# The second projection of a squared-ReLU MLP by seven block products in six of its eight chunks, on one core

## The reference, cut to what matters

```python
def squared_relu_mlp(x, w1, w2):
    return jnp.square(jax.nn.relu(x @ w1)) @ w2
...
x = x + squared_relu_mlp(rms_norm(x, mlp_norm[i]), mlp_w1[i], mlp_w2[i])
```

## Time and profile before

| what | value |
|---|---|
| time, median of 3 executions | 2232.59 us (2228.85 to 2233.13) |
| time of the profiled execution | 2230.44 us |
| its span | 2228.6 us |
| TensorE (PE) busy | 2059.4 us, 92% |
| VectorE (DVE) busy | 1388.8 us, 62% |
| ScalarE (ACT) busy | 978.0 us, 44% |
| GpSimd (POOL) busy | 328.4 us, 15% |
| mean granted TensorE clock | 0.969 of full speed |

### The profile page before, as it was taken

How to read it: one execution, slowest core, us unless ns; L and a number is a source line. 1 busy time by engine, 2 the same in 40 slices (tenths; PEclk the granted TensorE clock), 3 DMA queues, 4 the chain that set the end, 5 groups by cost and what they waited for, 6 DMA issues and landing times. The chain is left out here.

```text
span 2228.6 us, 28924 instructions
## 1 busy us (share of the span) xinstructions
PE 2059.4 (92%) x10963; PEld 1081.8 (49%) x10963; DVE 1388.8 (62%) x1507; ACT 978.0 (44%) x1257; POOL 328.4 (15%) x291
## 2 busy tenths in 40 slices
PE   7998988889399999999967999959899999999999
PEld 5445436644244544554435565544444444444444
DVE  5135227743789999999978452384696456555544
ACT  5122126732378888888856352272332212121210
POOL 0000021000123233233300000032020011011100
PEclk9999999999699999999988999979999999999999
DMA  6111220041289999999974552235202201210201
GB/s 269 38 38 39 67 57 1 1 180 79 106 349 415 408 413 406 395 399 409 390 288 181 174 193 80 79 91 187 76 1 76 76 38 38 75 75 0 75 0 76
DMA packets 74722, 353.03 MB, mean 158 GB/s; under 512 B 16336, under 2 KB 23120, under 8 KB 42064
## 3 DMA queue, kind: packets, MB, share of 16 engines
q1 hardware_dynamic: 56304, 305.21, 35.1%
q0 software_dynamic: 18336, 46.69, 6.5%
HBM read 326.67 MB, written 29.36 MB: 160 GB/s over the span
## 5 line engine op out<-in xcount | busy, mean ns | idle before, releaser
L413 PE MATMUL ps<-split,xt 128*128 128x512 f16 x928 | 353.9, 381 | 25.3 <-DMA xt<-arena 19.8
L414 PE MATMUL ps<-split,xt 128*128 128x512 f16 x928 | 353.8, 381 | 0.0
L415 PE MATMUL ps<-split,xt 128*128 128x512 f16 x928 | 353.7, 381 | 0.0
L544 DVE SCALAR_TENSOR_TENSOR split<-stage,split 128x2048 f16<-128x2048 f32 x128 | 289.4, 2282 | 5.7 <-ACT split L540 4.0
L540 ACT ACTIVATE split<-stage 128x2048 f16<-128x2048 f32 x128 | 240.5, 1904 | 94.4 <-PE ps L415 94.4
L413 PE MATMUL ps<-xt,split 128*128 128x512 f16 (+1 forms) x660 | 239.7, 363 | 9.9 <-issue 8.3
L414 PE MATMUL ps<-xt,split 128*128 128x512 f16 (+1 forms) x660 | 239.7, 363 | 0.0
L415 PE MATMUL ps<-xt,split 128*128 128x512 f16 (+1 forms) x660 | 239.4, 363 | 0.0
L413 PE MATMUL ps<-split,arena 128*128 128x512 f16 x512 | 194.1, 379 | 0.3 <-DVE resid L1901 0.3
L414 PE MATMUL ps<-split,arena 128*128 128x512 f16 x512 | 194.0, 379 | 0.0
L415 PE MATMUL ps<-split,arena 128*128 128x512 f16 x512 | 194.0, 379 | 0.0
(11 more groups left out here) (383 smaller groups left out, 3628.9 us busy)
## 6 DMA issues: line engine op xcount, KB each, us to landing
stage<-in_w_gate SPq DMA_DIRECT2D x64, 1024.0 KB, 7.5
stage<-in_w_up SPq DMA_DIRECT2D x64, 1024.0 KB, 7.9
arena<-in_w_down SPq DMA_DIRECT2D x64, 1024.0 KB, 7.9
stage<-in_w_mlp SPq DMA_DIRECT2D x32, 1024.0 KB, 6.3
arena<-in_conv_taps POOLq DMA_DIRECT2D x32, 576.0 KB, 4.3
stage<-in_w_dense_a SPq DMA_DIRECT2D x16, 1024.0 KB, 7.3
stage<-in_w_dense_b SPq DMA_DIRECT2D x12, 1024.0 KB, 9.6
resid<-in_x SPq DMA_DIRECT2D x16, 512.0 KB, 4.5
```

Source lines behind the costliest of these rows:

```text
L413: nc.tensor.matmul(out_ap, lh, rh, start=start, stop=False)
L414: nc.tensor.matmul(out_ap, lh, rl, start=False, stop=False)
L415: return nc.tensor.matmul(out_ap, ll, rh, start=False, stop=stop)
L544: nc.vector.scalar_tensor_tensor(out=wlo(s), in0=wstage(s), scalar=WS, in1=whi(s), op0=ALU.mult, op1=ALU.subtract).then_inc(s_wo[s], 1)
```

## The change

In chunks 1 to 6 the down part becomes a seven-product scheme too. Its operands are, on the side of the hidden features, the blocks `A11`, `A12`, `A22` (names of their place) and the sums `S1` to `S4` of blocks, and on the side of the weights `B11`, `B21`, `B22` and the sums `T1` to `T4`. Chunk 7 keeps a plain down part. What changes in detail:

- **TensorE.** A down part has 28 groups of 6 matmuls (7 products by 4 tiles) in place of 16 groups of 12. The bank of each is given by `DOWN_BANK`; a group waits for the read of its bank's last use (`bank_reader`), and the first group of each product also for the operands.
- **Weight operands.** The up and the down part each have seven, and share a ring of seven buffers (`RING`), so that an operand of one part may be written only when the product that used the buffer in the other part is done. `mlp_hi` and `mlp_lo` go out of chunks 1 to 7.
- **GpSimd.** Per chunk it has four more weight sums (`down_sums`), four sums of hidden blocks (`hidden_sums`) and the low parts of these four, 128 x 1024 each. At the end, in chunk 7, it has six sums of 128 x 2048.
- **VectorE.** The blocks of the result are not all added to `resid`. Three running sums `E_V`, `E_X`, `E_Y` take the products that several blocks share; GpSimd adds them to `resid` in chunk 7. There are 32 reads of a bank per down part in place of 16. `relu_square` and `hidden_lo` are 128 x 1024 in place of pairs of 128 x 512. `bank_sum` is a scalar_tensor_tensor that scales by `IWS`.
- **SyncE.** The two units of the up part and the two of the down part go to the same two `stage` slots. Those of the down part are loaded when the seven up operands are split, those of the next up part when the seven down operands are split.

```diff
+        DOWN_ORDER = ["B11", "B21", "T4", "T3", "B22", "T2", "T1"]
+        SUMS = [split[:, 12288:16384].bitcast(F32), stage[:, 4096:6144], stage[:, 6144:8192]]
+        H_OF = {"B11": "A11", "B21": "A12", "T4": "A22", "T3": "S3", "B22": "S4", "T2": "S2", "T1": "S1"}
+        DOWN_TO = {"B11": (H11, E_V), "B21": (H11,), "T4": (H21,), "T3": (E_X,), "B22": (H12,), "T2": (E_V,),
+                   "T1": (E_Y,)}
+        UP_BANK = [0, 1, 2, 3, 0, 1, 3]
+        DOWN_BANK = [0, 2, 1, 3, 2, 1, 0, 1, 2, 3, 0, 1, 2, 3]
...
+            def body(c):
+                for down in range(2):
+                    for s in range(2):
...
+                            sp.wait_ge(s_pl, 14 * (c - 1) + 7 * down)
+                        src = a["w_mlp"][bass.ds(SLOTS * c + 2 * down + s, 1), :, :].rearrange("o p c -> (o p) c")
+                        sp.dma_start(wstage(s), src).then_inc(s_wl[s], 16)
...
+            def hidden_sums(c):
+                pool.wait_ge(s_relu, 8 + 4 * (c - 1) + 4)
+                pool.wait_ge(s_ml, 8 + 3 * (c - 1) + 3)
+                add(U_X, U_V, U_X, ALU.add, s_hs)
+                pool.wait_ge(s_hs, 4 * (c - 1) + 1)
+                add(U_V, U_W, U_V, ALU.subtract, s_hs)
+                add(U_W, U_X, U_W, ALU.subtract, s_hs)
+                pool.wait_ge(s_hs, 4 * (c - 1) + 3)
+                add(U_Y, U_Y, U_W, ALU.subtract, s_hs)
+                pool.wait_ge(s_hs, 4 * (c - 1) + 4)
+                for name in ("S3", "S4", "S2", "S1"):
+                    pool.wait_ge(s_mh, 8 + 7 * (c - 1) + H_HI.index(name) + 1)
+                    add(h_slot(name)[:, 1024:2048], HQ[name], h_slot(name)[:, 0:1024], ALU.subtract, s_hp)
+
+            up_sums(1)
+            with pool.Fori(1, NC - 1) as c:
+                down_sums(c)
+                hidden_sums(c)
+                up_sums(c + 1)
+            pool.wait_ge(s_mr, PER * (NC - 2))
+            for n, (to, v0, v1) in enumerate([(H12, H12, E_V), (H12, H12, E_Y), (E_X, E_X, E_V), (H21, H21, E_X),
+                                            (E_X, E_X, E_Y), (H22, H22, E_X)]):
...
+                add(to, v0, v1, ALU.add, s_pool)
...
+                hidden_hi("A22")
...
+                    op_hi(act, 1, "T2", c)
+                    op_hi(act, 1, "T1", c)
+                    op_hi(act, 0, "A11", c + 1)
+                    hidden_hi("S3")
+                    hidden_hi("S4")
+                    hidden_hi("S2")
+                    hidden_hi("S1")
+                    for name in W_UP[1:]:
+                        op_hi(act, 0, name, c + 1)
...
+                    read("P5b", f)
+                    bank_sum(U_V, f, 6, U_V, "P3")
+                relu_square("A21", "P3")
...
+                    op_lo(dve, 1, "T1", c)
+                    for g in range(28):
+                        down_read(g)
+                        if g == 5:
+                            op_lo(dve, 0, "A11", c + 1)
+                        if g == 9:
+                            op_lo(dve, 0, "A12", c + 1)
+                        if g == 20:
+                            op_lo(dve, 0, "A22", c + 1)
+                    for name in W_UP[3:]:
+                        op_lo(dve, 0, name, c + 1)
...
+                    for g in range(28):
+                        name = DOWN_ORDER[g // 4]
+                        h, w = h_slot(H_OF[name]), w_slot(1, name)
+                        if g % 4 == 0:
+                            pe.wait_ge(s_pl, w_count(1, name, c))
+                            if H_OF[name] in H_LO_N:
+                                pe.wait_ge(s_hp, 4 * (c - 1) + H_LO_N[H_OF[name]])
...
+                        pe.wait_ge(s_mr, PER * (c - 1) + bank_reader(g))
```

More of the change, by code:

```diff
@@ L690, in build @@
[L690 to L694, removed]
+        RING = [split[:, 2048 * i:2048 * i + 2048] for i in range(4)] + [
+            Z[:, 0:1024].bitcast(F16), junk[:, :].bitcast(F16), Z[:, 1280:2304].bitcast(F16)]
+        W_UP = ["A11", "A12", "A22", "S2", "S3", "S1", "S4"]
+        W_DOWN = ["B11", "B21", "B22", "T4", "T3", "T2", "T1"]
@@ new lines, in build @@
+        W_LAST = ["B11", "B21", "B22", "B12"]
+        W_FROM = {"A11": (0, 0), "A12": (1, 0), "A22": (1, 1), "S2": (0, 0), "S3": (0, 1), "S1": (1, 1), "S4": (1, 0),
+                  "B11": (0, 0), "B21": (0, 1), "B12": (1, 0), "B22": (1, 1),
+                  "T3": (1, 1), "T1": (1, 0), "T2": (0, 0), "T4": (0, 1)}
+        SUM_N = {"S1": 1, "S3": 2, "S2": 3, "S4": 4, "T3": 1, "T1": 2, "T2": 3, "T4": 4}
+        UP_ORDER = W_UP
+        DOWN_ORDER = ["B11", "B21", "T4", "T3", "B22", "T2", "T1"]
@@ L1923, in _ @@
                 if j in (8, 9, 10):
-                    op_lo(dve, ("A11", "A12", "A22")[j - 8], 1)
+                    op_lo(dve, 0, W_UP[j - 8], 1)
                 if j in (11, 13):
@@ L1952, in body @@
                 for f in range(2):
                     dve.wait_ge(s_ua, 2 * (c - 1) + 1 + f)
-                    bank_sum(U_W, f, 1, U_V)
+                    bank_sum(U_W, f, 1, U_V, "P2")
+                relu_square("A11", "P2")
+                hidden_lo("A11")
+                for name in ("B11", "B21", "B22"):
+                    op_lo(dve, 1, name, c)
+                if last:
+                    op_lo(dve, 1, "B12", c)
                 for f in range(2):
-                    summed(0, f)
@@ L1965, in body @@
+                relu_square("A12", "P4")
+                hidden_lo("A12")
+                if not last:
+                    op_lo(dve, 1, "T4", c)
+                    op_lo(dve, 1, "T3", c)
+                for f in range(2):
+                    bank_sum(U_X, f, 5, U_X, "P5")
+                for f in range(2):
+                    bank_sum(U_V, f, 5, U_V, "P5b")
+                relu_square("A22", "P5")
+                hidden_lo("A22")
                 if not last:
-                    op_lo(dve, "A11", c + 1)
+                    op_lo(dve, 1, "T2", c)
@@ new lines, in body @@
+                if last:
+                    hidden_lo("A21")
+                    for j in range(8, 24):
+                        dve.wait_ge(s_pool, 4 + (0 if j < 16 and j % 2 == 0 else 2 if j < 16 else 6))
+                        down_sum(j, G_DOWN + j // 4 - 1)
+                else:
+                    op_lo(dve, 1, "T1", c)
[9 more added lines that the diff above has]
+                        op_lo(dve, 0, name, c + 1)
```

380 lines of the change are left out of this document (207 added, 173 removed).

## The result

The changed kernel takes 2265.22 us (median of 4 executions, 2262.03 to 2265.81), the kernel before 2232.05 us on the same chip (4 executions, 2228.85 to 2233.13): a ratio of 1.0148, 95% interval 1.0131 to 1.0166. It is 33 us slower. The forecast was 2257 us, the range 2238 to 2272. The profiled execution took 2265.81 us, its span is 2264.0 us.

What follows compares the result with a forecast made beforehand. TensorE's matmuls were taken to bound the MLP, with only TensorE's waits added. From 2230.4 us, plus 6.0 for six looped chunks (78.7 us each) and 20.2 for chunk 7, it forecast 2257 us, range 2238 to 2272.

Steps and rivals of the forecast that it cites:

- Sign and mechanism: Whole kernel: slower, chance 0.82, through TensorE's waits as GpSimd and VectorE take turns on SBUF operands.
- 24 matmuls less per chunk: Looped down part: 168 matmuls in place of 192, saving 5.2 us per chunk, 31.1 us in six.
- g8, 1.2 us: Looped down part, group g8: TensorE stalls 1.2 us for its bank, behind the first product's doubled reads.
- g12, 3.5 us: Looped down part, group g12: TensorE waits 3.5 us for S3, behind GpSimd's hidden sums and low part.
- g14, 1.3 us: Looped down part, group g14: TensorE waits 1.3 us for its bank, read late behind the next chunk's A12 low part.
- The clock, 0.2 us per chunk: Looped chunk, behind the 3.5 us wait: TensorE's lower clock adds 0.2 us, most of it hidden in the following wait.
- Chunk 7, 20.2 us: Chunk 7: GpSimd's six long sums delay VectorE; the down part starts 18.0 us late, the low clock costs 2.2 us.
- Ports shared: Rival, SBUF ports: VectorE's two-operand instructions run beside GpSimd's; chunk 75.5 us, total 2219 us, faster; chance 0.09.
- VectorE keeps its turns: Rival, mainly chunk 7: successive VectorE instructions keep GpSimd out; down part 10.8 us late, total 2249 us; chance 0.12.
- Turns fall worse: Rival, looped chunks: GpSimd ahead of T1 and low clock not hidden; 80.7 us each, total 2269 us; chance 0.15.
- The count alone: Rival, whole kernel: all waits hidden, only the matmul saving of 31.1 us counts, total 2199 us; chance 0.03.

Runs made afterwards that it cites:

- E8: Changed kernel with product B11 added to the output only, not to E_V, four reads per chunk less, result incomplete: 2267.91 us, ratio 1.0170 to the kernel before.
- E3: Changed kernel with 16 extra matmuls, result unused, ahead of group g12 of each looped down part: 2259.52 us, ratio 1.0126 to the kernel before.
- E6: Changed kernel with the order of E4 and the late short sums of E5 together: 2219.76 us, ratio 0.9948 to the kernel before.
- E4: Changed kernel, order alone changed: S3 first, S4's sum and the next chunk's A11 and A12 work moved behind: 2235.85 us, ratio 1.0020 to the kernel before.
- E5: Changed kernel with chunk 7's six long GpSimd sums cut into 24, begun behind its last square: 2248.23 us, ratio 1.0082 to the kernel before.
- E1: Changed kernel with chunk 7's six long GpSimd sums left out, result incomplete: 2249.86 us, ratio 1.0088 to the kernel before.
- E7: E6 with T1's low part moved behind read 11 and the next chunk's low parts further back: 2216.06 us, ratio 0.9940 to the kernel before.

## Why the prediction was right, and where it was off

- **Sign and mechanism** held: 2265.22 us lies in the range, 8 us over the forecast.
- **24 matmuls less per chunk** held: 337 records in the windows of a looped chunk, where the earlier trace rows have 361.
- **g8, 1.2 us, and g12, 3.5 us** measured 1.49 and 3.85. The two were 0.6 us too small together. As E8 shows they are one quantity, the lateness of S3's chain: forecast 4.7, measured 5.35. The order of the turns was right; S3 came at 56.8 in place of 56.4, and TensorE without its first wait would have come to g12 at 51.6 in place of 51.8.
- **g14, 1.3 us** was right in size (1.17 in E3), and not to be seen in the changed kernel.
- **The clock, 0.2 us per chunk** is the term whose working failed. The row it rested on showed the clock at 0.50 for 2.65 us behind a wait of 3.38. Half of a stretch of 2.65 us is lost, 1.3, and the step took it as hidden by g14's wait but for a little. With seven slow matmuls that is nearly so (1.5, where g14's wait would have been 1.2); with thirteen, in two chunks of six, it is 2.7. The mean over the six chunks is 2.0, where the forecast has 1.5 for g14's wait and the clock together. With the 0.6 us of the two waits a chunk comes to 79.9 in place of 78.7. That is 7.2 us in six chunks, a little over half of it by the two waits, of the 9.1 by which the account of the profiled execution was off.
- **Chunk 7, 20.2 us** measured 20.7. The down part starts 18.0 us late, as laid out: 9.47 and 5.80 us of waits, and 2.7 of slow matmuls between them, which the forecast had as wait (9.7 and 8.3). Those behind the second wait cost another 2.7, forecast 2.2.
- **Ports shared** is refuted: 5.53 us for a low part that needs 1.2 beside GpSimd's sum, where half of its pace would make some 2.4 (an estimate). The Trainium skill (SBUF — State Buffer, SBUF: two separate sides) says that the pair of ports is locked for a whole instruction; the trace agrees (5.37 and 5.53 us).
- **VectorE keeps its turns** is refuted by the same rows: the low parts from 2165.27 to 2176.17 follow one another without a wait for ScalarE, and GpSimd gets a whole sum between any two.
- **Turns fall worse** did not come: GpSimd stood behind `T1` in each chunk. Two chunks reached that rival's 80.7 us, by the clock.
- **The count alone** fell, by waits of 5.3 us per chunk in place of none. E6 comes nearer to it, at 75.05 us per chunk.

Where did the expected gain of 31 us go? Each looped chunk won 5.2 us and paid 5.3 in waits and some 2 by the clock; and chunk 7 paid 20.7, of which 16.5 for six sums put where VectorE needs the same ports. E4 and E5 take back both, and the rest of the gain, 10.5 us, can be measured. What stays open in chunk 7 is the wait of 2.5 us ahead of the down part (put down to VectorE's own chain, for which no experiment was made), and the clock behind it, which cost 1.7 us in E1 and E5 and nothing in E6 and E7.

## What to carry to other kernels

Where GpSimd works on SBUF and VectorE has both its operands there too, plan them as one engine that takes turns: add up the turns ahead of the first result that TensorE wants, put that result first, and give GpSimd's unhurried work the stretches in which VectorE only reads banks. When work on a helper engine takes over matmuls, what counts is not its busy time (GpSimd 24% here) but the length of the chain ahead of the first product that uses it. A wait of some us on TensorE can cost more than itself, for the matmuls behind it may run slowly; the order of E4, which turns waits of 1.49 and 3.85 us into 1.49, 0.57 and 0.43, won 4.9 us per chunk where the waits alone account for 2.9.

## What the runs showed of the hardware that was not expected

- Turns were strict even between instructions of VectorE that follow one another at once: in chunk 7 of the changed kernel one pair of a long sum and a low part per 5.45 us, three low parts in a row.
- An instruction that makes a float16 result out of one float32 and one float16 operand is somewhat cheaper on GpSimd: 2.12 us for 128x1024, beside 2.35 for float32 throughout.
- The granted clock behind a wait does not follow from the wait's length alone. Behind the same wait of 3.85 us it was low for seven or eight matmuls in four chunks and for thirteen or fourteen in two. Behind 9.5 us it was low for thirteen in the changed kernel and for nine in E3 and E4. Behind waits of 0.57 and 1.49 us (E4) it stayed at full. Behind 2.52 us (E1, and the same in E5) the first two matmuls ran at full and some eight after them slowly, 1.7 us in all; behind 2.53 us at the same place in E6 and E7 none did. What decides it was not settled.
